# Dilated attention by tiles of two heads, with the next tile's projections in pieces between the steps of its pairs

## The reference

```python
def _dilated_attention_mixer(x, w_qkv, w_out):
    B, S, _ = x.shape
    qkv = (x @ w_qkv).reshape(B, S, N_DIL_GROUPS, 3, N_HEADS, HEAD_DIM)
    ...
    for g, (window, dil) in enumerate(DIL_CONFIGS):
        o, l = _dilated_group(qkv[:, :, g, 0], qkv[:, :, g, 1], qkv[:, :, g, 2],
                              window, dil, slopes[g])
    ...
    wts = jax.nn.softmax(jnp.stack(lses), axis=0)
    o = jnp.sum(wts[..., None] * jnp.stack(outs), axis=0)
    return o.reshape(B, S, ATTN_WIDTH).astype(x.dtype) @ w_out
```

## Time and profile before

| | |
|---|---|
| Median of 3 runs | 3557.4 us (3556.03 to 3557.8) |
| Profiled execution | 3555.88 us, its span 3554.1 us |
| PE busy | 3406.6 us (96%) |
| POOL busy | 2509.9 us (71%) |
| DVE busy | 1494.2 us (42%) |
| ACT busy | 824.8 us (23%) |
| Granted TensorE clock | 0.990 of full on the mean |

### The profile page before, as it was taken

How to read it: one execution, slowest core, us unless ns; L and a number is a source line. 1 busy time by engine, 2 the same in 40 slices (tenths; PEclk the granted TensorE clock), 3 DMA queues, 4 the chain that set the end, 5 groups by cost and what they waited for, 6 DMA issues and landing times.

```text
span 3554.1 us, 48351 instructions
## 1 busy us (share of the span) xinstructions
PE 3406.6 (96%) x18548; PEld 2824.0 (79%) x18548; DVE 1494.2 (42%) x2315; ACT 824.8 (23%) x1463; POOL 2509.9 (71%) x2220
## 2 busy tenths in 40 slices
PE   7999989999999999989898999989999998999998
PEld 6887878888888888878787888877778787777876
DVE  6653463112311152341626213365756525565643
ACT  1110233110211022231324211121332312232321
POOL 7998787888788876447374788856556785656675
PEclk9999999999999999999999999999999999999999
DMA  5553222222232222112121232222222222222222
GB/s 183 186 186 114 79 86 92 94 92 94 87 94 93 98 89 90 48 60 83 37 95 37 86 102 95 88 86 72 66 60 69 78 89 81 66 67 71 59 89 72
DMA packets 322426, 312.06 MB, mean 88 GB/s; under 512 B 11568, under 2 KB 306128, under 8 KB 322000
## 3 DMA queue, kind: packets, MB, share of 16 engines
q1 hardware_dynamic: 304928, 277.91, 25.0%
q10 hardware_dynamic: 17328, 31.78, 2.7%
HBM read 307.56 MB, written 2.10 MB: 87 GB/s over the span
## 4 chain that ended last, share of the span: by engine, by line
PE 45%; issue 28%; POOL 20%; DVE 4%; ACT 1%; POOLq 0%; DMA 0%; SPq 0%; DVEq 0%; ACTq 0%
PE ps L1759 16%; POOL wh L346 14%; PE ps L384 12%; POOL wl L350 7%; PE ps L1515 4%; PE ps L557 3%; PE ps L1802 2%; PE ps L2335 1%; PE ps L859 1%; PE ps L531 1%; PE ps L2136 1%; DVE at_sc L1427 1%; PE ps L2107 1%; PE ps L2121 1%; DVE at_nb L1443 0%
## 5 line engine op out<-in xcount | busy, mean ns | idle before, releaser
L346 POOL TENSOR_TENSOR wh<-w_raw,zero 128x512 fp32r<-128x512 f32 (+3 forms) x1108 | 1146.7, 1045 | 1013.4 <-PE ps L384 460.4
L350 POOL TENSOR_TENSOR wl<-w_raw,wh 128x512 fp32r<-128x512 f32 (+3 forms) x1108 | 1420.9, 1293 | 0.0
L384 PE MATMUL ps<-xh,wh 128*128 128x512 f32 x1888 | 738.6, 391 | 6.8 <-DVE at_ol L1560 4.5
L384 PE MATMUL ps<-xh,wl 128*128 128x512 f32 x1888 | 734.9, 389 | 0.0
L384 PE MATMUL ps<-xl,wh 128*128 128x512 f32 x1888 | 734.8, 389 | 0.0
L384 PEld LDWEIGHTS ps<-xh,wh 128*128 128x128 f32 x1888 | 354.5, 188 | 83.2 <-ACT at_qk L1528 5.2
L384 PEld LDWEIGHTS ps<-xh,wl 128*128 128x128 f32 x1888 | 354.4, 188 | 74.0
L384 PEld LDWEIGHTS ps<-xl,wh 128*128 128x128 f32 x1888 | 354.6, 188 | 73.4 <-issue 1.0
L1117 DVE TENSOR_TENSOR ps<-sg,ps 128x512 f32<-128x512 f32 x88 | 61.2, 696 | 590.9 <-PE ps L384 563.2
L1759 PE MATMUL ps<-xh,wh 128*128 128x512 f32 x688 | 288.9, 420 | 5.4 <-POOL wl L350 2.6
L1759 PE MATMUL ps<-xh,wl 128*128 128x512 f32 x688 | 271.3, 394 | 0.0
(11 more groups left out here) (357 smaller groups left out, 6155.8 us busy)
## 6 DMA issues: line engine op xcount, KB each, us to landing
w_raw<-in_w_in SPq DMA_DIRECT2D x120, 512.0 KB, 4.1
w_raw<-in_ffn_w_gate SPq DMA_DIRECT2D x88, 512.0 KB, 4.7
w_raw<-in_ffn_w_up SPq DMA_DIRECT2D x88, 512.0 KB, 4.7
w_raw<-in_attn_w_qkv SPq DMA_DIRECT2D x72, 512.0 KB, 4.2
w_raw<-in_ffn_w_down SPq DMA_DIRECT2D x64, 512.0 KB, 3.6
ada_raw<-in_ada_w ACTq DMA_DIRECT2D x24, 512.0 KB, 3.9
stats<-in_ada_w ACTq DMA_DIRECT2D x24, 512.0 KB, 3.9
w_raw<-in_ffn_w_down SPq DMA_DIRECT2D x32, 384.0 KB, 4.0
```

The source lines that it names most:

```text
L346: done.append(s["w_hi"].up(pool.tensor_tensor(hi[:, parts[q]], raw[:, parts[q]], zero, ALU.subtract)))
L350: s["w_lo"].up(pool.tensor_tensor(lo[:, parts[q]], raw[:, parts[q]], hi[:, parts[q]].bitcast(F32), ALU.subtract))
L384: mm = self.nc.tensor.matmul(out, a[:, slot, w], b(t), start=start and t == order[0] and q == 0, stop=stop and t == order[-1] and q == 2)
```

## The change

The work goes by tiles of two heads instead of quads of four. The columns of `attn_w_qkv` are put in a new order on the host, so that a chunk holds queries and keys of one tile and one group (three chunks), then values of groups 0 and 1 (one chunk), and in even tiles a chunk with the values of group 2 for both tiles. That is still 36 chunks. Queries, keys and values have buffers by the tile's parity, and the values of group 2 of odd quads lie in the not yet used last tile of `at_oh` and `at_ol`.

After tile 0 has been projected, the projections of tile t+1 are issued in pieces between the steps of the pairs of tile t. A piece is three matmuls of 512 columns or six of 256, an eighth of a half. A pair's step has two halves (16 pieces), or three at the first two pairs of odd tiles: two pieces between the turns of the two heads, six between scores and output, the rest behind the output. During the last tile there are no projections left; there 14 pieces of the first output chunk (all of it but the eighth feature tile) are issued, three in a step.

Banks: the tile's output goes to bank 7 (`OUT`) for every tile, so its first output step waits for the last tile's `o_lo`. The turned probabilities use banks 5, 6 and again 5, so the second head's far transposes wait for ACT's copy of the first head's. ACT and DVE issue their parts in a matching order. DVE forms the low part of the keys one pair later than that of the queries where a step has two halves, and forms the biases for a tile, four instructions, at that tile's first pair.

```diff
-    def pe_out(self, pe, st, c1, xs, before=None, residue=False):
+    def pe_out(self, pe, st, c1, xs, before=None, residue=False, begun=0):
...
+                done = begun if pair == 0 else 0
+                self.product(pe, (c1 + pair) % 2, KT, 256, m * P, self.ps[:, n % 4], xs, start=not done, before=before if n == 0 else None, order=range(done, KT))
...
+        w = self.dram["attn_w_qkv"]
+        loads = [self.halves(w, 0, KT, (256 * c, 0), 256) for c in range(9 * QUADS)]
...
-    SCORES, SCORES_NEAR, TURNED = 2, 4, 5
+    SCORES, SCORES_NEAR, TURNED, OUT = 2, 4, 5, 7
...
+        return 9 * (tile // 2) + 5 * (tile % 2)
...
-        pe.wait_ge(s["lin_ev"].sem, st.at("lin_ev", 18 * quad + 16))
+        pe.wait_ge(s["lin_ev"].sem, st.at("lin_ev", 2 * self.tile_chunk(i // 4) + 6))
...
+        if hh == 0:
+            if i:
+                pe.wait_ge(s["pt_copied"].sem, st.at("pt_copied", 3 * i))
+            far()
+            near()
+        else:
+            near()
+            pe.wait_ge(s["pt_copied"].sem, st.at("pt_copied", 3 * i + 1))
+            far()
...
-        if i % QUAD_PAIRS == 0:
-            pe.wait_ge(s["lin_ev"].sem, st.at("lin_ev", 18 * (quad + 1)))
+        if i % 4 == 0:
+            pe.wait_ge(s["lin_ev"].sem, st.at("lin_ev", 2 * self.tile_chunk(i // 4 + 1)))
+            pe.wait_ge(s["o_lo"].sem, st.at("o_lo", i // 4))
...
-        s["pt_copied"].up(self.nc.scalar.activation(self.at_pt[:, n], self.ps[:, self.TURNED + n], ACT.Copy))
+        s["pt_copied"].up(self.nc.scalar.activation(self.at_pt[:, n], self.ps[:, self.TURNED + n % 2], ACT.Copy))
...
+        if j == (1 if tile else 2):
+            pe.wait_ge(s["qk_low"].sem, st.at("qk_low", 2 * tile + m + 1))
+        if j < 3:
+            for t in range(KT):
+                if arrive:
+                    arrive(t)
+                mm = self.piece(c % 2, 256, m * P, self.ps[:, m], self.x_parts(), (t,), t == 0, t == KT - 1)
+                if t == KT - 1:
+                    s["acc"].up(mm)
+                yield
+            return
...
+                if t % 2:
+                    yield
...
+    def pe_attn_begin_out(self, pe, st):
+        s, c = self.s, st.chunk0 + 9 * QUADS
+        arrive = self.arrival(pe, c, KT)
+        for m, ks in ((0, range(6)), (1, range(6)), (0, (6,)), (1, (6,))):
+            pe.wait_ge(s["lin_ev"].sem, st.at("lin_ev", 18 * QUADS - 1 + m))
+            for t in ks:
+                if m == 0:
+                    arrive(t)
+                pe.wait_ge(s["o_lo"].sem, st.at("o_lo", t + 1))
+                self.piece(c % 2, 256, m * P, self.ps[:, m], self.heads_out(), (t,), t == 0, False)
+                yield
...
+    def attn_halves(i):
+        tile, n = divmod(i, 4)
+        if tile + 1 >= KT:
+            return 0
+        return 2 if tile % 2 == 0 or n > 1 else 3
+    def pe_attn(self, pe, st):
+        s = self.s
+        self.pe_first(pe, st, True)
+        fill = self.pe_attn_project(pe, st, 0, 2)
+        for _ in range(3 * 8):
+            next(fill)
+        self.pe_attn_scores(pe, st, 0)
+        for _ in fill:
+            pass
+        for i in range(ATTN_PAIRS + 1):
+            tile = i // 4
+            pieces = 8 * self.attn_halves(i)
+            if pieces and i % 4 == 0:
+                fill = self.pe_attn_project(pe, st, tile + 1)
+            if i == ATTN_PAIRS - 4:
+                fill = self.pe_attn_begin_out(pe, st)
+            if i >= ATTN_PAIRS - 4:
+                pieces = 3
+            parts = (2, 6, pieces - 8) if pieces > 8 else (1, 1, 1)
+            if i:
+                self.pe_attn_turn(pe, st, i - 1, 0)
+            for _ in range(parts[0]):
+                next(fill, None)
+            if i:
+                self.pe_attn_turn(pe, st, i - 1, 1)
+            if i + 1 < ATTN_PAIRS:
+                self.pe_attn_scores(pe, st, i + 1)
+            for _ in range(parts[1]):
+                next(fill, None)
+            if i:
+                self.pe_attn_out(pe, st, i - 1)
+            for _ in range(parts[2]):
+                next(fill, None)
+        c1 = st.chunk0 + 9 * QUADS
+        self.pe_out(pe, st, c1, self.heads_out(), before=lambda t: pe.wait_ge(s["o_lo"].sem, st.at("o_lo", t + 1)), residue=True, begun=KT - 1)
...
+        for n in range(2 * self.tile_chunks(0)):
+            self.act_attn_half(act, st, 0, n // 2, n % 2)
+        for i in range(ATTN_PAIRS + 1):
+            tile, at = divmod(i, 4)
+            if i:
+                for n in range(3):
+                    self.act_attn_turned(act, st, i - 1, n)
+            if i < ATTN_PAIRS:
+                for hh in range(2):
+                    self.act_attn_probs(act, st, i, hh)
+            first = sum(self.attn_halves(4 * tile + k) for k in range(at))
+            for n in range(first, first + self.attn_halves(i)):
+                self.act_attn_half(act, st, tile + 1, n // 2, n % 2)
+                if n == 0 and i:
+                    self.act_attn_o_hi(act, st, tile - 1)
+            if at == 0 and i >= ATTN_PAIRS - 4:
+                self.act_attn_o_hi(act, st, tile - 1)
...
+        self.dve_attn_qk_low(dve, st, 0)
+        for i in range(ATTN_PAIRS + 1):
+            tile, at = divmod(i, 4)
+            if i < ATTN_PAIRS:
+                if at == 0:
+                    self.dve_attn_biases(dve, tile)
+                self.dve_attn_far(dve, st, i, 0)
+            if i:
+                self.dve_attn_norm(dve, st, i - 1, 1)
+            if at == 1 and self.attn_halves(i - 1) == 2:
+                self.dve_attn_qk_low(dve, st, tile + 1, (1,))
+            if i < ATTN_PAIRS:
+                self.dve_attn_near(dve, st, i)
+                self.dve_attn_far(dve, st, i, 1)
+                for hh in range(2):
+                    self.dve_attn_least(dve, st, i, hh)
+                self.dve_attn_norm(dve, st, i, 0)
+            if at == 0:
+                if tile + 1 < KT:
+                    self.dve_attn_qk_low(dve, st, tile + 1, (0,))
+                if tile:
+                    self.dve_attn_o_lo(dve, st, tile - 1)
+                if self.attn_halves(i) == 3:
+                    self.dve_attn_qk_low(dve, st, tile + 1, (1,))
...
+def attention_columns():
+    part = lambda g, kind, at, n: np.arange(n) + g * 3072 + kind * 1024 + at
+    out = []
+    for tile in range(KT):
+        out += [part(g, kind, P * tile, P) for g in range(3) for kind in range(2)]
+        out += [part(g, 2, P * tile, P) for g in range(2)]
+        if tile % 2 == 0:
+            out.append(part(2, 2, P * tile, 2 * P))
+    return np.concatenate(out)
```

More of the change, by code:

```diff
@@ L1313, in stage_attn @@
     def stage_attn(self, n):
-        w, loads = self.dram["attn_w_qkv"][0], []
-        for quad in range(QUADS):
-            loads += [self.halves(w, 0, KT, (g * 3072 + part * 1024 + quad * 256, 0), 256) for g in range(3) for part in range(3)]
+        w = self.dram["attn_w_qkv"]
+        loads = [self.halves(w, 0, KT, (256 * c, 0), 256) for c in range(9 * QUADS)]
         return add(ATTN, NORM), [(1, loads), self.out_chunks(self.dram["attn_w_out"][0])]
@@ L1381, in near @@
                 at = hh * 2 * P + g * P
-                mm = nc.tensor.transpose(ps[:, self.TURNED + 1, at:at + P], self.at_pr[:, hh, T + g * P:T + (g + 1) * P], self.identity[:])
+                mm = nc.tensor.transpose(ps[:, near_bank, at:at + P], self.at_pr[:, hh, T + g * P:T + (g + 1) * P], self.identity[:])
             if hh:
                 s["t_done"].up(mm)
-        for step in ((near, far) if hh else (far, near)):
-            step()
+        if hh == 0:
[3 more added lines that the diff above has]
+            near()
+        else:
+            near()
+            pe.wait_ge(s["pt_copied"].sem, st.at("pt_copied", 3 * i + 1))
+            far()
     def pe_attn_out(self, pe, st, i):
@@ L1473, in pe_attn_half @@
-        if j % 3 < 2:
-            self.product(pe, c % 2, KT, 256, m * P, self.ps[:, m], self.x_parts(), before=arrive)
-        else:
-            self.values(pe, c % 2, 256, 0, 256, m, *self.x_tiles(), before=arrive)
+        pe.wait_ge(s["lin_ev"].sem, st.at("lin_ev", n - 3 if (tile, j) == (0, 2) else n - 1))
+        if j == (1 if tile else 2):
[9 more added lines that the diff above has]
+            return
@@ new lines, in pe_attn_half @@
+        xh, xl = self.x_tiles()
+        for r in (2 * m, 2 * m + 1):
+            out = self.ps[:, m, (r % 2) * 256:(r % 2) * 256 + 256]
+            for t in range(KT):
+                if arrive and r == 2 * m:
+                    arrive(t)
+                w = slice(t * 256, t * 256 + 256)
+                for q, (x, b) in enumerate(((xh, self.wh), (xh, self.wl), (xl, self.wh))):
+                    mm = self.nc.tensor.matmul(out, x[t][:, r], b[:, c % 2, w], start=t == 0 and q == 0, stop=t == KT - 1 and q == 2)
+                if r % 2 and t == KT - 1:
+                    s["acc"].up(mm)
+                if t % 2:
+                    yield
@@ new lines, in pe_attn_project @@
```

(41 more changed lines are left out.)

139 lines of the change are left out of this document (43 added, 96 removed).

## The result

| | before | changed |
|---|---|---|
| median of the runs, us | 3556.89 | 3508.62 (3507.91 to 3510.36) |
| profiled execution, first to last instruction | 3554.1 | 3507.1 |
| part behind `pe_first` up to `pe_last` | 613.9 | 566.2 |
| waits of PE for at_pr and at_sc there | 35.3 | 1.1 |
| all named waits of PE there | 47.5 | 2.8 |

The ratio is 0.9865, 95% interval 0.9853 to 0.9877, so 48.3 us less. The forecast was 3508.5 us, and 565.0 us for the part. One run of experiment 4 took 3794.8 us at a granted clock of 0.844, and the time given there is the median of the other three.

The account below looks back on a forecast made before the run. DVE was taken to bound the pairs, PE the projections. 545.9 + 16.3 + 1.5 + 0.8 + 0.5 = 565.0 us against 613.9 is 48.9 less, so 3507.0 profiled and 3508.5 us median; range 3494 to 3530.

Parts of the forecast that it names:

- The bound: DVE sets the pace in the pairs, PE in the projections; 68.0 us of waits, edges and lower clock can be won.
- Nothing waits: Through all pairs PE starts matmuls without a wait; its waits for at_pr and at_sc are under 3 us together.
- PE sets the pace: In the last tile's steps PE needs 6.8 us, over DVE's 5.5 us, so PE decides the step's length.
- Changes of kind: Switching between pieces and scores, output or transposes costs PE 0.51 us a step, 32 times, 16.3 us.
- rival of free changes: Switching between kinds of matmul costs nothing, the 16.3 us fall away: 3492 us; chance 0.09.
- Biases: Four on DVE at a tile's edge take 4.2 us, once in four pairs, hidden by the pieces.
- low keys: Low part of the keys one pair later: PE may wait some 0.1 us in four tiles, 0.5 us in all.
- second turn: ACT's copy of bank 5 ends at 1.42 us, PE's far transposes come at 2.35 us; nothing waits.
- output bank: One bank waits for o_lo, formed a whole run of pieces ahead; the 1.51 us at a quad's edge go, three times.
- The last tile: Begun output product: a wait of 1.5 us for the last o_lo and about 0.8 us for POOL over both chunks.
- The sum: From behind pe_first to pe_last 565.0 us against 613.9, 48.9 us less; whole kernel 3508.5 us.
- Waits stay: Rival: links with little cover come late beside a busy POOL, 0.7 us in each of 32 steps: 3531 us; chance 0.18.

Follow-up runs that it names:

- experiment 4: Changed kernel with DVE forming the low part of the keys in the tile's first step for all tiles; 3518.36 us, ratio 0.989.
- 5 and 6: DVE's search for the least score done twice for each head, in the changed kernel (3510.73 us) and in the kernel of before (3599.01 us).
- Experiment 1: Changed kernel with all pieces of the next tile in the step of a tile's first pair, none in the other three; 3530.16 us, ratio 0.9925.
- experiment 7: Changed kernel with a step's pieces in two groups, 2 between the turns, the others between scores and output, none behind the output; 3521.43 us, ratio 0.9899.
- experiment 9: Changed kernel with two of a step's pieces moved into the middle of the twelve output matmuls, in 28 steps; 3517.34 us, ratio 0.9887.
- experiment 2: Changed kernel with the two pieces between the two heads' turns moved behind the scores; 3525.69 us, ratio 0.9911.

## Why the prediction was right

- **The bound.** PE followed DVE in the pairs; shown by 5 and 6. Experiment 1 shows it from the other side for three steps of each tile. The prediction set out "18.1 + 10.8 us of waits"; it left out 6.4 us for `at_pr` at L1376 and 6.1 us for `at_pt`, which went with the others. They are in its 68.0 us, so the sum does not suffer.
- **Nothing waits.** Forecast: under 3 us together for `at_pr` and `at_sc`; 1.1 us came. Both waits stand in one step of the last tile. There "PE sets the pace" failed once: with one piece behind the output, the eviction of `at_oh`, its low part, far scores and division come late, the chain of experiment 7. That step took 8.0 us instead of 6.8; the other two with scores took 6.7.
- **Changes of kind.** From the first turn of the second step (1366.29) to the first of the last tile (1826.46) pass 460.2 us. The 40 halves of keys and queries, 20 of values and 27 pairs in them are 217.6 + 115.2 + 114.5 = 447.3 us by the prediction's bare durations, so 12.9 us or 0.48 us a step are left, where 0.51 stood in the sum. A step of keys and queries loses 0.51 (15.63 - 10.88 - 4.24), one of values 0.37 (16.13 - 11.52 - 4.24). The rival of free changes falls: 3492 us would have followed. The Trainium skill ("TensorE: Matmul & The Clock Gate", Part 3) says that weights are loaded ahead of running matmuls; the trace agrees inside a run of pieces and into transposes, and not at the other changes. The weights of the piece's matmul at 1383.41 are loaded from 1383.18 and those of the transposes at 1382.06 from 1381.83, 0.23 us ahead. But a group's first matmul has its weights loaded from 1382.61 for 1382.63 and from 1392.07 for 1392.08, and scores and output begin together with their first load (1384.84, 1390.61). That this is the cause of the price was not tested. "Into transposes none shows" was wrong behind an output, by 0.06 us (7). And "0.11 us into pieces, 0.09 us ahead of output" was not the whole price of a group: experiment 9 shows 0.34, with 0.14 of it in the output block, which the bare duration already held. The sum was right because that block is there once in either kernel.
- **Biases, low keys, second turn, output bank.** All were hidden, as forecast. At the second turn PE came to the far transposes 2.25 us after the turn's start (2.35 forecast), and experiment 2 shows that the copy ends some 1.3 us after it (1.42 forecast). Without the two pieces the loss is 17 us (2), with the low keys a pair earlier 10 us (4). For the low keys 0.5 us was in the sum and nothing came. For the output bank the prediction named "a whole run of pieces ahead". Taking that run away (7) costs 13 us, but not by a wait for the bank: there is none, and the loss comes through the queues of ACT and DVE, a chain that the prediction did not name. The cover of the biases was not taken away by itself.
- **The last tile.** The wait of 1.51 us for `at_ol` came as forecast. PE's wait for POOL ahead of `pe_last` is 0.23 us, where 0.8 stood: the third chunk's split began at 1872.79 and the last of its instructions ended at 1884.08, 11.3 us in all, as forecast.
- **The sum.** 565.0 forecast, 566.2 measured: 0.9 us less for changes, 0.5 and 0.6 less for low keys and POOL, 1.1 more for the two waits; some 2 us remain. Of these 1.5 lie behind 1826.46: up to `pe_last` pass 57.7 us, of which the bare durations are 18.3 for pairs and 32.6 for output weights, the waits 2.8 and the five steps' changes 2.5 at 0.51; where in that stretch is open. So errors of some 2 us on either side cancel, and the sum came closer than its terms. The part also begins 0.8 us later than before (1317.93 against 1317.13), so the whole span lost 47.0 us (3554.1 to 3507.1) and not 47.7; nothing was given back behind the part. That 3508.5 met 3508.62 to 0.1 us is luck: the profiled execution was taken as 1.5 us below its median, as before, but lies 0.3 above it, and this makes up for what the span lacked of 48.9 us.
- **Waits stay.** The division grew longer with POOL at work beside it: its mean over the part rose from 692 to 1004 ns, while the search for the least score stayed at 948 ns. With 15 us in a step it costs nothing, as this rival's own working allowed.

## What to carry to other kernels

Put independent work of the full engine between the links of a chain that another engine paces, in every step: in one lump a tile, nearly half of the gain was lost. Then find for each link what stands between its start and the place where PE needs it, and what stands ahead of it in the other engines' queues; here the tightest place was where the step's last result and the tile's last result meet in one queue. Work behind a step's last product is cover as much as work ahead of it, and regrouping it to save a tenth of a microsecond can cost a whole one.

## What had not been expected of the hardware

- The same short stand of PE was followed by either level of the granted clock. After four waits of 1.85 us (experiment 4) it fell twice, to 0.59 on the mean of 4 us in the one shown, where the scores took 0.97 us more, and stayed at 1.00 twice. After three pairs of waits of 1.24 and 1.07 us (experiment 7) it was 1.00 once, 0.57 once and 0.68 once. So a wait can cost more than itself, and its length alone doesn't tell when.
- An output block of 24 matmuls takes 1.46 us and two of 12 take 0.80 us each: 0.14 us for one more beginning and end, which no row shows as idle time.
- Where the kind changes into pieces, scores or output, no weights are loaded ahead in this trace: a load leads its matmul by 0.23 us inside a run of pieces, and by 0.02 us at most at the first of a group.
